# Attention in three layers: groups interleaved by a written order, ada steps moved into the product, filler matmuls on TensorE

## The chip, the cores and the metric

One Trainium2 chip, one of its cores. The engines are TensorE (PE), VectorE (DVE), ScalarE (ACT), GpSimd (POOL) and SyncE (SP, which here issues the weight loads). Each has its own queue that it works off in order; they meet only by semaphores. The metric is the device time of one execution in microseconds (us). TensorE's clock has two levels here, 1.2 and 2.4 GHz; a granted clock of 0.50 in the profile is the lower, 1.00 the upper.

## The reference, cut to what matters

The program is a chain of a block with two layers and a block with one, on 256 tokens of width 1024, all in float32:

```python
for l in range(2):                                    # first block
    mod = silu(c) @ ada_w[l] + ada_b[l]               # shifts, scales, gates
    hn = adaln(x, mix_norm_g[l], sh_m, sc_m)
    a_q, ..., d_v = split(hn @ w_in[l], IN_SPLITS)    # 1024 -> 3016
    o_a = diff_attention(...)             # A: p0 - lam*p1, then rmsnorm per head
    o_b = latent_attention(...)           # B: rmsnorm, @ w_uq, @ w_ukv, rope
    o_c = indexed_sparse_attention(...)   # C: index scores (I), top 64 keys, attention
    o_d = chunk_band_attention(...)       # D: banded bias
    x = x + g_m * (concat(o_a, o_b, o_c, o_d) @ w_out[l])
    x = x + g_f * (swiglu(...) if l == 0 else moe_swiglu(...))
x = rmsnorm(x, final_norm_g)
# second block: ffn1; qkv product; 8 heads of neighbourhood attention (N) and
# 8 of dilated attention (L); output product; ffn2
```

Each of A, B, C, D has 4 heads of 64 columns. A query block is 128 tokens; its keys are the first 128 or all 256.

## The kernel before, in words

**Weights.** Weight chunks of 1 MB come through a ring of six in one stream. A chunk is two pieces. For each piece ACT writes a rounded high part (`split_hi`, L988), DVE the low part (`split_lo`, L1411), and PE multiplies high*high, high*low and low*high (L527 to L529). Four pieces (`SPLITS`) are in work at once, so DVE can be that far ahead of PE. The products before attention are `gemm(0)`, `gemm(2)` and `gemm(4)`; the first runs from about 56 to 118.8 us.

**The modulation (ada).** 48 chunks of 1 MB are reduced on DVE by `ada_step` (L1324, L1327, L1330, two instructions each) into rows. POOL issues their loads (L444) into two slots of their own; a load waits until the step two before it has been done. Chunks 0 to 7 are done at the start, 8 to 25 inside attention 0, the rest in the first feed-forward part.

**Attention.** The work is cut into units: a kind (A, I, B, C, D in layers 0 and 1; N and L in the wide layer 2), a query block b and a part. A01 is kind A, block 0, part 1. Names that only have a kind and a number (C2, B6) are fills. A unit goes through:

- fill: PE transposes queries and keys into PSUM bank 7 (L642; for B also products, L678, L684), ACT copies them out (L1071);
- `score` on PE (L719), for one unit into one of two PSUM pairs;
- `bias` on DVE: scale and bias (L1497), row maximum (L1500);
- `probabilities` on ACT: four exponentials (L1117), for I a relu (L1112);
- for A the two parts are combined on DVE (`finish`, L1542, L1547); for I the weighted sum (`index_add`, L1511) and eight rounds of maximum and replace that select 64 keys (L1521, L1522);
- `values` on PE: transposes of the probabilities (L731), a copy by ACT (`copy_pT`, L1124), products with the values (L743);
- `store` on DVE (L1557; for A a norm with a root on POOL).

All engines run through one list of units: in each layer group A (A00 A01 A10 A11), then B, then C (I00 I01 I10 I11 C00 C10), then D. In each turn of PE's loop the score of the next unit stands before the values of this one; the fills of the next group stand around them. On DVE `prepare` and `prepare_rope` do the norms and rotations of the next group, and in layer 0 one ada step follows each unit. So at most one unit is ahead of the one whose values are being made.

## Time and profile before

| | us |
|---|---|
| median of 3 runs | 2490.25 (2489.54 to 2490.9) |
| profiled execution, device time | 2481.82 |
| its span | 2480.1 |
| PE busy | 2131.3 (86%) |
| DVE busy | 1693.4 (68%) |
| ACT busy | 1344.9 (54%) |
| POOL busy | 46.2 (2%) |

The page gives busy time by engine, then the span in 40 slices, of 62 us each. Slices 3 to 5 hold attention 0, 10 to 12 attention 1, and 35 and 36 the attention of layer 2. The long stretch of nines between is the experts. A matmul's end is modelled, so PE's busy time is a little more than its work. A PE row with `x8` is eight hardware records; four float32 matmuls of the program make eight.

### The profile page before, as it was taken

The numbers are of one execution on the slowest core, as the hardware profiler recorded it, in microseconds if no ns is written. First come the engines' busy times: TensorE is split into PE (matmuls) and PEld (weight loads), VectorE is DVE, ScalarE is ACT, GpSimd is POOL, SyncE is SP. The second block draws the span as 40 slices with busy tenths as digits, with TensorE's granted clock in tenths as the row PEclk, the third lists the DMA queues.
The fourth block names the chain that finished last, engine by engine and source line by source line (L and its number), as shares of the span: only waits on it lengthen the run. The fifth ranks groups of instructions, "written<-read, shape, count | busy, mean of one in ns | idle before, by whom it ended". The sixth has DMA issues, their size and how long they took to land.

```text
span 2480.1 us, 26703 instructions
## 1 busy us (share of the span) xinstructions
PE 2131.3 (86%) x9538; PEld 1735.1 (70%) x9538; DVE 1693.4 (68%) x2020; ACT 1344.9 (54%) x1832; POOL 46.2 (2%) x80
## 2 busy tenths in 40 slices
PE   3944779978657799999999999999969997866997
PEld 3733658866445688888888888888848885655886
DVE  5378377753463689898989898989975545344554
ACT  2422244434331687878787878787844434343443
POOL 1010000000000000000000000000000000000000
PEclk9956789989557899999999999999979998858999
DMA  9543358734003599999999999999954553202551
GB/s 374 180 152 104 130 208 314 308 140 159 0 15 146 214 358 353 351 353 351 353 351 354 352 356 349 355 349 356 373 204 169 189 182 120 84 17 86 202 186 51
DMA packets 80598, 573.41 MB, mean 231 GB/s; under 512 B 9088, under 2 KB 9728, under 8 KB 12272
## 3 DMA queue, kind: packets, MB, share of 16 engines
q1 hardware_dynamic: 70112, 508.59, 54.4%
q0 software_dynamic: 7936, 57.05, 6.2%
q10 hardware_dynamic: 2448, 6.41, 0.7%
q8 instruction: 63, 1.03, 0.2%
q14 instruction: 39, 0.32, 0.0%
HBM read 570.97 MB, written 1.05 MB: 231 GB/s over the span
## 4 chain that ended last, share of the span: by engine, by line
PE 73%; issue 12%; DVE 9%; ACT 3%; DMA 2%; POOL 1%; ACTq 0%; POOLq 0%; DVEq 0%
PE ps L527 21%; PE ps L529 21%; PE ps L528 21%; PE ps L743 2%; PE ps L719 2%; PE ps L822 1%; PE ps L829 1%; DMA arena<-in_ada 1%; PE ps L797 1%; PE ps L642 1%; DVE ps L1497 1%; DVE Z L1330 1%; PE ps L731 1%; DVE xt_low L1404 1%; DVE arena L1522 1%
## 5 line engine op out<-in xcount | busy, mean ns | idle before, releaser
L1670 DVE TENSOR_TENSOR weights_low<-ring,weights_high 128x1024 fp32r<-128x1024 f32 x672 | 803.8, 1224 | 63.1 <-ACT weights_high L1153 49.1
L1153 ACT ACTIVATE weights_high<-ring 128x1024 fp32r<-128x1024 f32 x672 | 710.5, 1060 | 105.4 <-PE ps L529 92.4
L527 PE MATMUL ps<-weights_high,xt_high 128*128 128x512 f32 x1808 | 729.7, 404 | 36.6 <-DVE xt_low L1404 24.7
L529 PE MATMUL ps<-weights_high,xt_low 128*128 128x512 f32 x1808 | 712.6, 394 | 0.0
L528 PE MATMUL ps<-weights_low,xt_high 128*128 128x512 f32 x1808 | 712.4, 394 | 0.0
L1411 DVE TENSOR_TENSOR weights_low<-ring,weights_high 128x1024 fp32r<-128x1024 f32 x294 | 357.7, 1224 | 244.0 <-ACT weights_high L988 242.5
L988 ACT ACTIVATE weights_high<-ring 128x1024 fp32r<-128x1024 f32 x294 | 307.3, 1057 | 335.9 <-PE ps L529 320.7
L527 PEld LDWEIGHTS ps<-weights_high,xt_high 128*128 128x128 f32 x1808 | 345.0, 191 | 110.8 <-DVE xt_low L1404 26.9
L529 PEld LDWEIGHTS ps<-weights_high,xt_low 128*128 128x128 f32 x1808 | 344.0, 190 | 73.7
L528 PEld LDWEIGHTS ps<-weights_low,xt_high 128*128 128x128 f32 x1808 | 345.5, 191 | 68.4 <-issue 1.0
L527 PE MATMUL ps<-weights_high,hT_high 128*128 128x512 f32 x712 | 283.4, 398 | 5.5 <-DVE hT_low L1448 4.2
L529 PE MATMUL ps<-weights_high,hT_low 128*128 128x512 f32 x712 | 277.3, 389 | 0.0
L528 PE MATMUL ps<-weights_low,hT_high 128*128 128x512 f32 x712 | 277.1, 389 | 0.0
L527 PEld LDWEIGHTS ps<-weights_high,hT_high 128*128 128x128 f32 x712 | 133.7, 188 | 36.9 <-DVE hT_low L1448 5.0
L528 PEld LDWEIGHTS ps<-weights_low,hT_high 128*128 128x128 f32 x712 | 133.7, 188 | 30.6 <-issue 3.4
L529 PEld LDWEIGHTS ps<-weights_high,hT_low 128*128 128x128 f32 x712 | 133.6, 188 | 28.1
L519 PE MATMUL ps<-unit,XN 128*128 128x128 f32 x160 | 36.5, 422 | 87.5 <-DVE XN L1378 80.4
L743 PE MATMUL ps<-arena 128*128 128x64 f32 x320 | 67.7, 395 | 34.8 <-ACT arena L1124 16.4
L519 PEld LDWEIGHTS ps<-unit,XN 128*128 128x128 f32 x160 | 32.7, 227 | 91.6 <-DVE XN L1378 83.8
L743 PEld LDWEIGHTS ps<-arena 128*128 128x128 f32 x320 | 63.6, 302 | 43.2 <-ACT arena L1124 30.1
L731 PE MATMUL ps<-unit,arena 128*128 128x128 f32 x160 | 36.1, 394 | 58.6 <-ACT arena L1117 43.4
L1117 ACT ACTIVATE arena<-ps,nmax 128x256 f32<-128x256 f32 (+1 forms) x112 | 47.1, 436 | 58.7 <-DVE nmax L1500 58.6
(192 smaller groups left out, 1474.1 us busy)
## 6 DMA issues: line engine op xcount, KB each, us to landing
ring<-in_stream SPq DMA_DIRECT2D x483, 1024.0 KB, 4.9
Z<-in_ada POOLq DMA_DIRECT2D x42, 1024.0 KB, 5.1
arena<-in_ada POOLq DMA_DIRECT2D x6, 1024.0 KB, 16.4
Z<-in_na POOLq DMA_DIRECT2D x1, 2048.0 KB, 7.8
Z<-in_dil POOLq DMA_DIRECT2D x1, 2048.0 KB, 12.2
band<-in_band ACTq DMA_DIRECT2D x2, 768.0 KB, 18.7
X<-in_x SPq DMA_DIRECT2D x1, 1024.0 KB, 5.4
gate_mix<-in_rows ACTq DMA_DIRECT2D x2, 512.0 KB, 9.6
```

Of the source, the lines that this page charges most:

```text
L519: m = nc.tensor.transpose(ps[:, j, (kt % 2) * T + b * P:(kt % 2) * T + (b + 1) * P], XN[:, b, kt * P:(kt + 1) * P], ident[:, :])
L527: nc.tensor.matmul(out, xh, wh, start=n, stop=False, skip_group_check=True)
L528: nc.tensor.matmul(out, xh, wl, start=False, stop=False, skip_group_check=True)
L529: return nc.tensor.matmul(out, xl, wh, start=False, stop=last, skip_group_check=True)
L719: m = nc.tensor.matmul(out, lhs, rhs, start=True, stop=True)
L731: m = nc.tensor.transpose(ps[:, 4 + h // 2, (h % 2) * T + kb * P:(h % 2) * T + (kb + 1) * P], src[:, head_slot(h), kb * P:(kb + 1) * P], i ...
L743: m = nc.tensor.matmul(ps[:, 6, h * HD:(h + 1) * HD], PT[:, h, kb, :], PROJ[:, kb, c:c + HD], start=kb == 0, stop=kb == u.nk // P - 1)
L988: act.activation(WH[:, p % SPLITS, :], ring[:, chunk % RING, half * PIECE:(half + 1) * PIECE], ACT.Copy).then_inc(hi_ready, 1)
L1117: ins = act.activation(PR[:, par, s, 0:u.nk], src[:, s, 0:u.nk], ACT.Exp, bias=nmax[:, par, s:s + 1], accum_out=den[:, par, h:h + 1])
L1153: act.activation(WH[:, slot, :], raw, ACT.Copy).then_inc(m["hi_ready"], 1)
L1411: nc.vector.tensor_tensor(WL[:, p % SPLITS, :], ring[:, chunk % RING, half * PIECE:(half + 1) * PIECE], WH[:, p % SPLITS, :].bitcast(F32), ...
L1670: nc.vector.tensor_tensor(WL[:, slot, :], raw, WH[:, slot, :].bitcast(F32), ALU.subtract).then_inc(m["lo_ready"], 1)
```

## The change

1. The rule that built one list of units is gone. PE, ACT and DVE each have a sequence written out by hand for layers 0 and 1, and a loop for layer 2. `Order` objects give every fill, score, transposition and so on its number within its semaphore. Groups now overlap: I (index scores) runs inside A, the selection of block 0 beside B's fills, B and D before C.
2. Scratch that groups shared gets places of its own in the x^T buffers, which are idle in attention (`xt_words`). PSUM stays as it was.
3. `values` is split into `turn` and `values`. Each has six bf16 matmuls of constants into parts of PSUM that nobody reads (`stay_busy`), before its last wait: 12 for each of 24 units, 288 in all.
4. Of the 18 ada steps of attention 0, 14 go into `gemm_lo(0)` on DVE: ten behind every second split, four behind the last.
5. `combine` folds the four scalings of p0 away: it forms p0 + p1 * (r1 * lam * den0), and the division by den0 is done at the store.
6. The memset of `KI4` goes from DVE to POOL. The A store's norm is cut in two (`store_squares`, `store_normed`) so that the root is not waited for.

```diff
 class Order:
+    def __call__(self, layer, name):
+        return self.start(layer) + self.names(layer).index(name) + 1
+FILLED = Order("A0 A1 C3 C2 B0 B1 B2 B3 B4 B5 C0 B6 B7 B8 B9 D0 D1 C1", "N00 N01 N10 N11 L00 L01 L10 L11")
+SCORED = Order("A00 A01 I00 I01 A10 A11 I10 I11 B00 B10 D00 D10 C00 C10", "N00 N10 N01 N11 L00 L10 L01 L11")
...
+            def stay_busy(count, bank):
+                for _ in range(count):
+                    nc.tensor.matmul(ps[:, bank, 256:512], busy[:, 0:P], busy[:, 0:256], start=True, stop=True,
+                                     skip_group_check=True)
...
+            def turn(layer, name):
+                if TURNED(layer, name) > 1:
+                    pe.wait_ge(pT_ready, TURNED(layer, name) - 1)
+                stay_busy(6, 5)
+                if u.kind == "A":
+                    pe.wait_ge(combined, COMBINED(layer, name))
+                else:
+                    pe.wait_ge(probs, WEIGHED(layer, name))
...
+            def values(layer, name):
+                if TURNED(layer, name) > 1:
+                    pe.wait_ge(mixed, TURNED(layer, name) - 1)
+                stay_busy(6, 6)
+                pe.wait_ge(pT_ready, TURNED(layer, name))
...
             def gemm_lo(g):
                 for p in range(SPLITS, 4 * GEMM_GROUPS[g]):
                     split_lo(GEMM_CHUNK[g] + p // 2, p % 2)
+                    if g == 0 and p % 2 == 1:
+                        ada_step(ADA_EARLY + (p - SPLITS) // 2)
+                if g == 0:
+                    lambda_sums()
+                    for a in range(2 * GEMM_GROUPS[g] - SPLITS // 2, ADA_IN_GEMM):
+                        ada_step(ADA_EARLY + a)
...
+            def combine(layer, b):
+                dve.wait_ge(probs, WEIGHED(layer, f"A{b}1"))
+                link(nc.vector.reciprocal(rden[:, 0, :], den[:, n1, :]))
+                link(nc.vector.scalar_tensor_tensor(rden[:, 0, :], rden[:, 0, :], lamc[:, 4 + layer:5 + layer], den[:, n0, :],
+                                                    ALU.mult, ALU.mult))
...
+            def attention(layer):                       # DVE, layers 0 and 1
+                prepare_index(layer)
+                more_ada(0)
+                bias(layer, "A00")
+                bias(layer, "A01")
+                norm_latent(layer)
+                more_ada(1)
+                if layer == 0:
+                    lambdas()
+                combine(layer, 0)
+                index_add(layer, "I00")
+                index_add(layer, "I01")
+                bias(layer, "A10")
+                store_squares(layer, "A01")
+                bias(layer, "A11")
+                rope_latent(layer)
+                combine(layer, 1)
+                select_keys(layer, 0)
...
+                select_keys(layer, 1)
+                store(layer, "B10")
+                bias(layer, "C00")
+                store(layer, "D00")
+                bias(layer, "C10")
+                store(layer, "D10")
+                more_ada(2)
+                store(layer, "C00")
+                more_ada(3)
+                store(layer, "C10")
```

Where the instructions stand. First DVE's queue where the first product ends and attention 0 begins (L1411 is a split, L1324, L1327 and L1330 are ada steps, L1497 and L1500 the bias of A00, L1360 and L1602 the norm of B), before:

```order
L1411 TENSOR_TENSOR weights_low<-ring,weights_high 128x1024 x22
...
L1782 TENSOR_SCALAR gdiff<-gdiff 128x64
L1497 SCALAR_TENSOR_TENSOR ps<-ps,alibi 128x4x128
L1500 TENSOR_REDUCE nmax<-ps 128x4
L1360 TENSOR_SCALAR rstd<-ss 128x2 x2
L1602 TENSOR_SCALAR arena<-arena,rstd 128x256 x2
L1602 TENSOR_SCALAR arena<-arena,rstd 128x128 x2
L1324 TENSOR_SCALAR Z<-Z,csilu 128x1024
L1330 SCALAR_TENSOR_TENSOR Z<-Z,csilu 128x1024
L1327 SCALAR_TENSOR_TENSOR Z<-Z,csilu 128x1024
L1330 SCALAR_TENSOR_TENSOR Z<-Z,csilu 128x1024
```

and in the changed kernel (L1497 is now the split, L1404, L1407 and L1410 the ada steps, L1706 and L1707 `prepare_index`, L1589 and L1592 the bias):

```order
L1497 TENSOR_TENSOR weights_low<-ring,weights_high 128x1024 x2
L1407 SCALAR_TENSOR_TENSOR Z<-Z,csilu 128x1024
L1410 SCALAR_TENSOR_TENSOR Z<-Z,csilu 128x1024
...
L1407 SCALAR_TENSOR_TENSOR Z<-Z,csilu 128x1024
L1410 SCALAR_TENSOR_TENSOR Z<-Z,csilu 128x1024
L1706 TENSOR_SCALAR w<-arena 128x8
L1707 COPY xt_words<-arena 128x128
L1706 TENSOR_SCALAR w<-arena 128x8
L1707 COPY xt_words<-arena 128x128
L1407 SCALAR_TENSOR_TENSOR Z<-Z,csilu 128x1024
L1410 SCALAR_TENSOR_TENSOR Z<-Z,csilu 128x1024
L1589 SCALAR_TENSOR_TENSOR ps<-ps,alibi 128x4x128
```

What moved: the splits have ada steps between them and behind them, and one more stands before the first bias; the long run of ada steps behind B's norm is gone.

Second, PE's queue in the last part of attention 0, from the scores of C (L719 score, L731 transposes, L743 values, L519 the transposes of the next product), before:

```order
L719 MATMUL ps<-arena 128x128 x4
L719 MATMUL ps<-arena 128x256 x4
L731 MATMUL ps<-unit,arena 128x128 x4
L743 MATMUL ps<-arena 128x64 x4
L719 MATMUL ps<-arena 128x128 x4
L731 MATMUL ps<-unit,arena 128x128 x8
L743 MATMUL ps<-arena 128x64 x8
L719 MATMUL ps<-arena 128x256 x4
L731 MATMUL ps<-unit,arena 128x128 x4
L743 MATMUL ps<-arena 128x64 x4
L731 MATMUL ps<-unit,arena 128x128 x8
L743 MATMUL ps<-arena 128x64 x8
```

and the end of the same part in the changed kernel (L482 `stay_busy`, L674 score, L689 transposes, L705 values, L490 as L519):

```order
L689 MATMUL ps<-unit,arena 128x128 x4
L674 MATMUL ps<-arena 128x128 x4
L482 MATMUL ps<-unit 128x256 x6
L689 MATMUL ps<-unit,arena 128x128 x8
L482 MATMUL ps<-unit 128x256 x6
L705 MATMUL ps<-arena 128x64 x4
L674 MATMUL ps<-arena 128x256 x4
L482 MATMUL ps<-unit 128x256 x6
L705 MATMUL ps<-arena 128x64 x8
L482 MATMUL ps<-unit 128x256 x6
L689 MATMUL ps<-unit,arena 128x128 x4
L482 MATMUL ps<-unit 128x256 x6
```

What moved: C is now last, and a score or another unit's step stands between the transposes and the values of nearly every unit, with six fillers before each.

Third, two turns of PE's loop in layer 2 (L642 and L603 are fills), before:

```order
L642 MATMUL ps<-unit,arena 128x128 x8
L731 MATMUL ps<-unit,arena 128x128 x8
L743 MATMUL ps<-arena 128x64 x8
L719 MATMUL ps<-arena 128x256 x4
L731 MATMUL ps<-unit,arena 128x128 x8
L743 MATMUL ps<-arena 128x64 x8
L719 MATMUL ps<-arena 128x256 x4
```

and now:

```order
L689 MATMUL ps<-unit,arena 128x128 x8
L674 MATMUL ps<-arena 128x256 x4
L603 MATMUL ps<-unit,arena 128x128 x4
L482 MATMUL ps<-unit 128x256 x6
L705 MATMUL ps<-arena 128x64 x8
L482 MATMUL ps<-unit 128x256 x6
L689 MATMUL ps<-unit,arena 128x128 x8
L674 MATMUL ps<-arena 128x256 x4
L603 MATMUL ps<-unit,arena 128x128 x4
L482 MATMUL ps<-unit 128x256 x6
L705 MATMUL ps<-arena 128x64 x8
```

What moved: the score now stands behind the transposes of a unit two earlier, no longer one.

## Rows read from the trace of the kernel before

**Rows 1.** The page: granted clock in tenths, in 40 slices.

```profile
PEclk9956789989557899999999999999979998858999
```

**Rows 2.** Windows (us): busy time of each engine; attention 0, 1, 2, first product.

```profile
core 0: us, PE busy (x) PEld busy (x) DVE busy (x) ACT busy (x) POOL busy (x), PEclk, DMA share, GB/s
56.00:118.80 62.80, 62.75 (x277) 51.63 (x275) 25.48 (x25) 26.07 (x31) 0.00 (x0) 1.00 0.51 186
118.80:270.00 151.20, 75.38 (x320) 55.44 (x320) 103.98 (x215) 41.59 (x126) 12.76 (x21) 0.56 0.36 130
607.70:736.70 129.00, 73.28 (x321) 55.23 (x321) 60.79 (x173) 41.53 (x126) 3.02 (x3) 0.60 0.02 6
2127.00:2216.30 89.30, 69.87 (x332) 57.33 (x330) 25.04 (x33) 31.17 (x86) 0.00 (x0) 0.67 0.04 13
```

**Rows 3.** Timeline: start us, us, engine line op; in brackets idle before; layer 1.

```profile
701.38 1.11 PE L731 MATMUL ps<-unit,arena 128*128 128x128 f32 x4 [8.73 <-ACT arena L1117]
...
724.56 1.23 DVE L1497 SCALAR_TENSOR_TENSOR ps<-ps,band 128x1024 f32<-128x1024 f32 x1 [8.20 <-PE ps L719]
```

**Rows 4.** Timeline: where attention 1 and attention 2 begin.

```profile
607.73 1.09 ACT L1008 ACTIVATE arena<-ps 128x512 f32<-128x512 f32 x2 [8.85 <-PE ps L529]
...
612.85 0.70 DVE L1497 SCALAR_TENSOR_TENSOR ps<-ps,alibi 128x512 f32<-128x512 f32 x1 [13.68 <-PE ps L719]
...
2138.04 0.66 PE L642 MATMUL ps<-unit,arena 128*128 128x128 f32 x4 [1.18 <-ACT arena L1008]
```

**Rows 5.** DVE's groups of attention 0: count, busy us, mean ns, idle before.

```profile
L1330 DVE SCALAR_TENSOR_TENSOR Z<-Z,csilu 128x1024 f32<-128x1024 f32 x18 | 23.1, 1285 | 0.6
L1327 DVE SCALAR_TENSOR_TENSOR Z<-Z,csilu 128x1024 f32<-128x1024 f32 x13 | 16.7, 1285 | 3.3 <-DMA Z<-in_ada 2.8
...
L1324 DVE TENSOR_SCALAR Z<-Z,csilu 128x1024 f32<-128x1024 f32 x5 | 3.8, 751 | 2.8 <-DMA Z<-in_ada 2.7
```

**Rows 6.** DMA issues of the whole span: count, KB each, median us to landing.

```profile
Z<-in_ada POOLq DMA_DIRECT2D x42, 1024.0 KB, 5.1
arena<-in_ada POOLq DMA_DIRECT2D x6, 1024.0 KB, 16.4
```

**Rows 7.** DVE's groups of attention 1.

```profile
L1542 DVE TENSOR_SCALAR arena<-arena,rden 128x256 f32<-128x256 f32 x4 | 1.1, 347 | 0.0
...
L1542 DVE TENSOR_SCALAR arena<-arena,rden 128x128 f32<-128x128 f32 x4 | 0.9, 281 | 0.0
```

**Rows 8.** Timeline of PE: values, scores and transposes at both levels of the clock.

```profile
660.75 3.67 PE L743 MATMUL ps<-arena 128*128 128x64 f32 x16 [1.11 <-ACT arena L1124]
...
682.06 2.00 PE L743 MATMUL ps<-arena 128*128 128x64 f32 x16 [1.11 <-ACT arena L1124]
...
2173.80 1.13 PE L719 MATMUL ps<-arena 64*128 64x256 f32 x8
2174.86 1.09 PE L731 MATMUL ps<-unit,arena 128*128 128x128 f32 x8
...
2181.27 2.08 PE L719 MATMUL ps<-arena 64*128 64x256 f32 x8
...
2192.62 2.08 PE L719 MATMUL ps<-arena 64*128 64x256 f32 x8
```

**Rows 9.** Timeline of PE: two passes of a weight product at half clock.

```profile
746.07 0.63 PE L529 MATMUL ps<-weights_high,xt_low 128*128 128x512 f32 x1
746.50 0.63 PE L527 MATMUL ps<-weights_high,xt_high 128*128 128x512 f32 x1
```

**Rows 10.** Windows of 4 us in attention 1 (columns as in rows 2).

```profile
628.00:632.00 4.00, 3.72 (x8) 1.95 (x10) 0.00 (x0) 0.98 (x5) 0.00 (x0) 0.50 0.00 0
632.00:636.00 4.00, 3.07 (x10) 0.99 (x8) 2.88 (x5) 1.93 (x9) 0.00 (x0) 0.95 0.00 0
...
664.00:668.00 4.00, 4.00 (x13) 3.17 (x13) 0.01 (x1) 0.00 (x0) 0.00 (x0) 0.50 0.00 0
...
696.00:700.00 4.00, 0.00 (x0) 0.00 (x0) 3.82 (x7) 0.18 (x1) 0.00 (x0) 0.50 0.00 0
```

More of the change, by code:

```diff
@@ L166, with __init__, names, start @@
-GROUPS, UNITS = attention_plan()
+    def __init__(self, kind, b, part):
+        self.kind, self.b, self.part = kind, b, part
+        self.name = f"{kind}{b}{part}"
+        self.half = part if kind in "NL" else 0
+        self.nk = T if kind in "NL" else P * (b + 1)
+UNIT = {u.name: u for kind in "ABICDNL" for b in range(NB) for part in range(2) for u in [Unit(kind, b, part)]}
+class Order:
+    def __init__(self, early, late=""):
+        self.early, self.late = early.split(), late.split()
+    def names(self, layer):
+        return self.early if layer < LAYERS else self.late
+    def start(self, layer):
+        return layer * len(self.early)
+    def end(self, layer):
+        return self.start(layer) + len(self.names(layer))
+    def __call__(self, layer, name):
+        return self.start(layer) + self.names(layer).index(name) + 1
@@ L167, with place @@
+COMBINED = Order("A01 A11")
+INDEXED = Order("I00 I01 I10 I11")
+def place(layer, name):
+    return SCORED.names(layer).index(name)
 N_CONST = 8
@@ L486, in _ @@
             root(0, 2)
-            attention_roots()
+            pool.wait_ge(gemm_out, 2 * sum(GEMM_GROUPS[:2]) + 2)
+            pool.memset(KI4, 0.0).then_inc(ki_cleared, 1)
+            root(0, 4)
+            for b in range(NB):
+                root(4, 8)
             pool.wait_ge(mod_ready, 12)
@@ L747, in attention @@
             def attention(layer):
-                us = units_of(layer)
                 pe.wait_ge(gemm_out, 2 * sum(GEMM_GROUPS[:2 * layer + 1]))
-                fills(us[0].g, 0, us[0].g.n_fills)
-                score(us[0])
-                for n, u in enumerate(us):
-                    part = fill_part(u)
-                    if part and last_of_group(u):
-                        fills(*part)
-                    if n + 1 < len(us):
-                        score(us[n + 1])
-                    if part and not last_of_group(u):
-                        fills(*part)
-                    if u.pu is not None:
-                        values(u)
+                fill(layer, "A0")
@@ new lines, in attention @@
+                fill(layer, "A1")
+                score(layer, "A00")
+                fill_index_keys(layer)
+                score(layer, "A01")
+                fill(layer, "C2")
+                fill(layer, "B0")
+                score(layer, "I00")
+                score(layer, "I01")
+                fill_latent_keys(layer)
+                turn(layer, "A01")
+                latent_queries(layer, 0)
+                score(layer, "A10")
+                latent_queries(layer, 1)
+                values(layer, "A01")
@@ new lines, in attention @@
+                score(layer, "B10")
+                fill(layer, "D1")
+                values(layer, "A11")
+                score(layer, "D00")
+                turn(layer, "B00")
+                score(layer, "D10")
+                values(layer, "B00")
+                turn(layer, "B10")
+                fill(layer, "C1")
+                values(layer, "B10")
+                turn(layer, "D00")
+                score(layer, "C00")
+                turn(layer, "D10")
+                values(layer, "D00")
@@ new lines, in attention @@
+                rope_latent(layer)
+                combine(layer, 1)
+                select_keys(layer, 0)
+                index_add(layer, "I10")
+                store_normed(layer, "A01")
+                index_add(layer, "I11")
+                bias(layer, "B00")
+                bias(layer, "B10")
+                store_squares(layer, "A11")
+                bias(layer, "D00")
+                store_normed(layer, "A11")
+                bias(layer, "D10")
+                store(layer, "B00")
```

622 lines of the change are left out of this document (310 added, 312 removed).

## The prediction

> **What bounds the kernel now.** I read the page first: engine shares and slices. PE is busy 86% of the span, and the slices in which it is not are few; in the same slices the granted clock drops [rows 1]. I then cut the time into stretches by a table of windows. The first weight product (56 to 118.8 us) is bound by PE: 62.75 of 62.8 us at full clock, DVE only 25.48 us busy, DMA share 0.51. The three attention stretches are bound by nothing for long: in layer 0 PE is busy 75.38 of 151.2 us, DVE 103.98, ACT 41.59; in layer 1 PE 73.28 of 129, DVE 60.79, ACT 41.53; and the granted clock averages 0.56 and 0.60, mostly the 1.2 GHz level [rows 2]. The timeline of layer 1 shows why: units take turns. While DVE does the key selection of C, PE stands idle 8.73 us, and soon afterwards DVE waits 8.20 us for the next score [rows 3]. So latency of one unit after another bounds these stretches, and a slow PE is in that chain. The windows of layers 0 and 1 begin with the product's last copy (1.09 us) and end with the last store; behind the copy they last 151.2 - 1.1 = 150 and 129.0 - 1.1 = 128 us, and layer 2 from its first fill at 2138.0 to 2216.3, 78 us [rows 2, 4]; together 356. All other stretches keep their instructions.
>
> **Part 1: 14 ada steps leave attention 0.** There 18 steps stand in DVE's queue: 23.1 + 16.7 + 3.8 = 43.6 us, 2.4 us each, and 2.8 + 2.7 us of waits for their loads [rows 5]. Four stay. Fourteen (34 us) go into the first product: ten behind every second split, four behind the last. The product asks DVE for 25.48 us in 62.8, so one step per pair of splits gives 2 x 1.23 + 2.4 = 4.9 us of DVE per 24 matmuls of 62.75/277 = 0.227 us, that is 5.4 us of PE [rows 2]: it fits by 0.5 us, and SPLITS = 4 pieces stand between DVE and PE. The cover is thin but real. The DMA share would be 0.51 + about 0.5. An ada load lands after 5.1 us (median of 42 here) and has two step periods less a step, 10.9 - 2.4 = 8.5 us, to do so; the bound above is the 16.4 us of the first six loads, which were issued together [rows 6]. I take the 5.1, and 2 us of loss in the product for contention (range 0 to 40, below).
> The four steps behind the last split are not covered. Two ring slots and 5.1 + 2.4 us per pair of steps make about 3.8 us a step: DVE comes to the first bias of attention 0 about 8 us late, and to the first combine about 10 us late (a fifth step, more_ada(0), also waits for its load). ACT's exponentials and I00's score wait behind that combine. Of the other steps, more_ada(1) is inside that figure and the last two stand in gaps at the end. Cost: 10 us.
>
> **Part 2: the new orders, layer 1, by DVE's queue.** Head: bias A00 starts 4.0 us after the copy as now (612.85 against 607.73 + 1.09) [rows 4]; then A00's and A01's exponentials, the combine and the two relus pass through one after another, and DVE starts index_add(I00) about 14.5 us after the copy (my estimate from the same operations' durations). From there DVE's queue has work that is ready nearly always: the scores are issued one or two units earlier, and the selections, the rope and the squares fill what were waits. DVE's 60.79 us of now [rows 2] lose the eight scalings of combine, 1.1 + 0.9 us [rows 7], the memset that moves to POOL and two copies: about 57. About 6 of these stand in the head, so 51 follow, plus some 2 us of issue gaps and one wait: 53. Tail behind bias C10: four exponentials, transposes, copy, values, store, 7.5 us at full clock. Sum 14.5 + 53 + 7.5 = **75 us, if PE runs at 2.4 GHz**.
> Does PE fit? Its 73.28 us at a mean clock of 0.60 are 44 us at full clock [rows 2], and the prices confirm the factor of nearly two: values 3.67 against 2.00 us, scores 2.08 against 1.13 [rows 8]. The new filler matmuls have no row. A 128x256 bf16 pass has half the columns of the 512-column passes: 0.227/2 = 0.113 us at full clock, and (746.50 - 746.07)/2 = 0.21 us at 1.2 GHz [rows 2, 9]; it could cost as little as nothing, where it lies in a wait, and 0.43 if width did not matter. I take 0.113 and 0.21. 96 of them are 11 or 20 us a layer. PE: 44 + 11 = 55 us of 75 at full clock, under DVE; but 88 + 20 = 108 at half clock, over DVE, and with the head's idle time the stretch is then 114.
> Which clock? From 628 to 632 us PE was busy 3.72 of 4 us at 0.50, and in the next 4 us the clock was 0.95; at 696 to 700 PE was idle and it was 0.50 again [rows 10]. In the new order PE has its gaps in the head (clock falls, as now) and from some 16 us on is busy 70 to 100%: at half clock it saturates, so the clock rises; at full clock it waits for DVE a quarter of the time and may fall again. I take 10 us over the 75: **85 us, a gain of 43** (bounds: 53 and 14).
> Layer 0 is the same plus the 10 us of part 1: **95 us against 150, a gain of 55** (bounds 65, 26).
>
> **Part 3: layer 2.** Now a unit takes 11.35 us (score to score at half clock: 2181.27 to 2192.62 [rows 8]). The new loop scores two units ahead, so PE never waits for an exponential: per unit at full clock transposes 1.09, score 1.13, fill 0.66 (first four units), values 2.00 [rows 4, 8] and fillers 12 x 0.113: 6.2 us with a fill, 5.6 without, a little less where ends overlap. ACT, by my estimate 4.7 us a unit, is shorter. A head of 9 us, the units (5.9 and 5.3 us, the last two without a score), a tail of 4: 52 us. At 1.2 GHz the sum per unit is 2.0 + 2.08 + 1.1 + 3.67 + 12 x 0.21 = 11.4, no shorter than today, and the stretch would take 91. PE without gaps should get its clock; I allow 4 us for the start: **56 us against 78, a gain of 22** (bounds 26 and -13).
>
> **Sum.** 55 + 43 + 22 - 2 = 118 us. Profiled execution 2481.8 - 118 = 2363.8. The median of the runs shown is 2490.25, 8.4 us above that execution, so the same gain gives **2372 us**. About 5 us (0.2%) is what can be told from no change.
>
> **A rule against the change.** The Trainium skill (TensorE: Matmul & The Clock Gate, Part 4, PE-mode transpose) says that transposes don't count as PE activity for the clock gate; fills and turns are transposes here, so less of PE's work would hold the clock than its busy time suggests. By that rule the time is the first rival's, 2465; by the busy rows it is 2372. No row here separates the two: most stretches hold both kinds.
>
> **Rivals.**
> - *The clock stays at 1.2 GHz* (20%). PE becomes the bound with its fillers on top: 124, 114 and 91 us for the three stretches, 329 against 356: gain 27, less 2: 2465. For: at 664 to 668 us PE was busy 4.00 of 4 us and the clock stayed at 0.50 [rows 10]. Against: gaps end now every busy spell, and the new queues leave hardly any.
> - *The clock stays up* (17%): 85, 75, 52 us: gain 144, less 2: 2348.
> - *Ada loads crowd the first product* (6%). If they land after 16.4 us [rows 6], a step takes (16.4 + 2.4)/2 = 9.4 us against 5.4 of PE: ten steps hold the splits 40 us, five more cost some 20: gain 58, 2432.
> - *Slower* (4%): the order hides nothing, since three in-order queues with cross waits merely exchange which engine stands; then all 288 fillers lie on the path at 1.2 GHz, 288 x 0.21 = 61 us, against 34 us of ada steps gone: 27 slower, 2517. It decides where the new overlap saves less than 27 us in three stretches. Against it: the idle times of rows 3 have nothing behind them but order.
> - *No net change* (2%): a mix of the two before.
>
> **How the numbers follow.** My forecast has 51%, around 2372 with its own range of 2350 to 2400. The five cases above take the rest. Eight in ten: from 2340 (full clock and a little) to 2445 (crowded loads, part of the low-clock case). Faster by over 0.2%: 0.51 + 0.20 + 0.17 + 0.06 and nearly nothing else, 0.94; same 0.02; slower 0.04.
>
> **What would show it.** Windows of the three stretches: lengths near 95, 85, 56 us; DVE busy near 70 us of layer 0 and 57 of layer 1, over two thirds of each; granted clock above 0.8 from 16 us into each. No PE wait over 3 us on DVE's selection. In the first product DVE busy near 50 us with PE still near 100%; a wait of DVE on the ada DMA just before prepare_index. I am wrong if the fillers are at 0.21 us and PE is busy all of the attention, if the first product is over 5 us longer, or if DVE still waits for scores in the middle of the stretches.

## The result, and the profile after

| | before | changed kernel |
|---|---|---|
| median of 4 runs each, same chip | 2489.89 us (2485.77 to 2490.9) | 2347.64 us (2345.06 to 2348.61) |
| ratio | | 0.943, 95% interval 0.9414 to 0.9446 |
| profiled execution, its span | 2481.82, 2480.1 us | 2348.61, 2346.6 us |

The predicted time was 2372 us, with a range of 2340 to 2445; the likeliest case's own range of 2350 to 2400 was missed by 2 us, on the fast side. The rival "the clock stays up" had said 2348.

The page's clock line, after, answers to [rows 1]:

```profile
PEclk9978799988979999999999999999979998987999
```

The table of windows, after: the three attention stretches, each from the end of the last copy of the product ahead of it to the end of its last store:

```profile
core 0: us, PE busy (x) PEld busy (x) DVE busy (x) ACT busy (x) POOL busy (x), PEclk, DMA share, GB/s
119.87:209.17 89.30, 63.07 (x416) 50.20 (x416) 72.35 (x183) 39.45 (x125) 7.83 (x11) 0.83 0.24 85
549.12:626.51 77.39, 61.00 (x416) 49.28 (x416) 56.86 (x164) 39.12 (x124) 3.02 (x3) 0.89 0.03 9
2028.23:2081.36 53.13, 47.47 (x384) 39.99 (x384) 23.70 (x32) 28.92 (x81) 0.00 (x0) 0.97 0.00 1
```

Measured in the same way the kernel before has 150.1, 127.8 and 78.3 us at clocks of 0.56, 0.59 and 0.63 (the longer windows of [rows 2]). The three gains are 60.8, 50.4 and 25.2 us, 136.4 in all; the profiled executions differ by 133.2, so the rest of the program is 3 us longer (1.1 us between attention 0 and 1, 0.4 between 1 and 2, 1.4 behind 2; why is not shown). The first product still ends its last copy at 119.87 us, as before, though DVE and the DMA engines have much more to do in it. Over the 62.8 us of [rows 2] DVE is now busy 51.12 us (it was 25.48) and the DMA share is 0.91 (it was 0.51). Its last three slices of 20 us:

```profile
60.00:80.00 20.00, 20.00 (x90) 16.58 (x89) 17.58 (x15) 9.40 (x12) 1.64 (x3) 1.00 0.85 327
80.00:100.00 20.00, 20.00 (x89) 16.55 (x89) 17.10 (x16) 9.56 (x12) 2.11 (x4) 1.00 0.99 385
100.00:120.00 20.00, 18.75 (x83) 15.22 (x82) 16.37 (x19) 6.22 (x9) 2.11 (x4) 1.00 0.95 369
```

Behind it stands the tail of ada steps. The timeline of DVE: where the last two steps of the tail begin, the step behind `prepare_index` (`more_ada(0)`), the first bias:

```profile
121.75 0.75 DVE L1404 TENSOR_SCALAR Z<-Z,csilu 128x1024 f32<-128x1024 f32 x1 [1.14 <-DMA Z<-in_ada]
...
129.70 1.28 DVE L1407 SCALAR_TENSOR_TENSOR Z<-Z,csilu 128x1024 f32<-128x1024 f32 x1 [5.88 <-DMA Z<-in_ada]
...
132.64 1.28 DVE L1407 SCALAR_TENSOR_TENSOR Z<-Z,csilu 128x1024 f32<-128x1024 f32 x1
...
135.15 0.69 DVE L1589 SCALAR_TENSOR_TENSOR ps<-ps,alibi 128x512 f32<-128x512 f32 x1
```

The bias starts 15.3 us behind the product's end. In the kernel before these were 4.3 us (124.13 less 119.87).

The wait of 5.88 us is for the load that POOL issued at 120.91 us. The rows of that issue and of the times to landing of the ten loads from 95 to 150 us:

```profile
120.91 0.53 POOL L410 DMA_DIRECT2D Z<-in_ada  x1 [3.73 <-DVE Z L1410]
...
DMA to landing us min/median/max: 4.9/5.1/8.8
```

120.91 + 8.8 is 129.7, where the step begins: this load took 8.8 us to land and not 5.1. ACT had issued a load of 384 KB (`in_uq`) at 120.29 us, which took 9.2 us (3.3 before). So some 3.7 us of the late start look like loads in each other's way; no run separates that.

What bounds layer 1 now? The timeline of DVE: three waits of the head, then every row that begins with an idle time of 0.2 us or more, and the row maximum of the last bias (start us, us, engine, line, operation; in brackets the idle time and who ended it):

```profile
553.74 0.70 DVE L1589 SCALAR_TENSOR_TENSOR ps<-ps,alibi 128x512 f32<-128x512 f32 x1 [4.08 <-PE ps L674]
...
560.61 0.18 DVE L1626 RECIPROCAL rden<-xt_words 128x4 f32<-128x4 f32 x1 [1.40 <-ACT arena L1151]
...
566.08 0.35 DVE L1606 SCALAR_TENSOR_TENSOR xt_words<-arena,w,cmask 128x128 f32<-128x128 f32 x1 [3.85 <-ACT arena L1146]
...
588.49 0.48 DVE L1606 SCALAR_TENSOR_TENSOR xt_words<-arena,w,cmask 128x256 f32<-128x256 f32 x1 [0.60 <-ACT arena L1146]
...
615.32 1.23 DVE L1589 SCALAR_TENSOR_TENSOR ps<-ps,alibi 128x1024 f32<-128x1024 f32 x1 [0.23 <-PE ps L674]
...
617.85 1.22 DVE L1592 TENSOR_REDUCE nmax<-ps 128x4 f32<-128x1024 f32 x1
...
621.45 0.42 DVE L1646 TENSOR_TENSOR XN<-ps,rden 128x256 f32<-128x256 f32 x1 [1.75 <-PE ps L705]
...
626.09 0.42 DVE L1646 TENSOR_TENSOR XN<-ps,rden 128x256 f32<-128x256 f32 x1 [4.13 <-PE ps L705]
```

From the first index_add (566.08) to the end of the last bias (619.07) DVE waits 0.83 us in 53.0. The waits of 8 to 9 us of [rows 3] are gone; PE's longest wait in this stretch is now one of 2.98 us:

```profile
580.02 0.64 PE L603 MATMUL ps<-unit,arena 128*96 128x128 f32 x4 [2.98 <-DVE xt_words L1689]
```

What is left is a head of 17.0 us and a tail of 7.4 us in which the units pass through one by one. The windows of head, dense part and tail show where the clock is low:

```profile
549.12:566.08 16.96, 12.61 (x65) 10.35 (x66) 5.98 (x21) 10.91 (x38) 1.01 (x1) 0.60 0.12 39
566.08:619.07 52.99, 42.54 (x302) 33.67 (x301) 49.35 (x139) 24.95 (x78) 2.01 (x2) 0.97 0.01 1
619.07:626.51 7.44, 5.85 (x50) 5.26 (x50) 1.53 (x7) 3.26 (x10) 0.00 (x0) 1.00 0.00 0
```

The clock is 0.60 in the head and 0.97 in the dense part, in which PE is busy 42.5 of 53.0 us.

Layer 2, the timeline of PE, one unit and the start of the next (L482 the fillers):

```profile
2061.87 1.04 PE L689 MATMUL ps<-unit,arena 128*128 128x128 f32 x8
2062.84 1.13 PE L674 MATMUL ps<-arena 64*128 64x256 f32 x8
2063.90 0.83 PE L482 MATMUL ps<-unit 128*128 128x256 bf16 x6
2064.57 1.90 PE L705 MATMUL ps<-arena 128*128 128x64 f32 x16
2066.30 0.82 PE L482 MATMUL ps<-unit 128*128 128x256 bf16 x6
2066.96 1.04 PE L689 MATMUL ps<-unit,arena 128*128 128x128 f32 x8
```

No row has an idle time in front: here PE is the bound, with 5.09 us a unit (it was 11.35 at half clock, [rows 8]). Of them 0.67 + 0.66 us are fillers (from the start of a group of six to the next row), 0.11 us for each filler. (A row's own 0.82 us overlaps the next one.)

### The profile page after: what moved, and what is told of

Its sections match the earlier page's. It is cut to its first block, busy times and chain, and to the rows that moved or that the text cites. A ratio compares the mean times of both kernels' runs of the same rounds, so it can differ in the third digit from the quotient of the medians.

```text
span 2346.6 us, 27245 instructions
## 1 busy us (share of the span) xinstructions
PE 2094.9 (89%) x9826; PEld 1714.2 (73%) x9826; DVE 1683.8 (72%) x2002; ACT 1342.4 (57%) x1832; POOL 48.1 (2%) x82
## 4 chain that ended last, share of the span: by engine, by line
PE 74%; issue 12%; DVE 8%; DMA 2%; ACT 2%; POOL 1%; ACTq 0%; POOLq 0%; DVEq 0%
PE ps L498 22%; PE ps L500 22%; PE ps L499 22%; PE ps L838 1%; PE ps L674 1%; PE ps L845 1%; DMA arena<-in_ada 1%; PE ps L813 1%; PE ps L705 1%; DVE xt_low L1490 1%; PE ps L603 1%; PE ps L482 1%; DVE ps L1589 1%; DMA Z<-in_ada 1%; DMA Z<-in_dil 1%
## 5 line engine op out<-in xcount | busy, mean ns | idle before, releaser
L1497 DVE TENSOR_TENSOR weights_low<-ring,weights_high 128x1024 fp32r<-128x1024 f32 x294 | 357.5, 1223 | 227.8 <-ACT weights_high L1004 226.4
L490 PE MATMUL ps<-unit,XN 128*128 128x128 f32 x160 | 34.4, 404 | 87.5 <-DVE XN L1464 80.1
L490 PEld LDWEIGHTS ps<-unit,XN 128*128 128x128 f32 x160 | 31.1, 217 | 91.4 <-DVE XN L1464 83.6
L1024 ACT ACTIVATE arena<-ps 128x512 f32<-128x512 f32 x48 | 25.7, 586 | 68.7 <-PE ps L500 68.7
L1242 ACT ACTIVATE hT_high<-ps 128x256 fp32r<-128x256 f32 x112 | 42.8, 382 | 37.7 <-PE ps L813 37.7
L1042 ACT ACTIVATE FS<-ps 128x512 f32<-128x512 f32 x33 | 19.7, 598 | 76.5 <-PE ps L500 76.5
L1812 DVE TENSOR_TENSOR hT_low<-ps,hT_high 128x256 fp32r<-128x256 f32 x112 | 46.9, 418 | 22.9 <-ACT hT_high L1242 22.9
## 6 DMA issues: line engine op xcount, KB each, us to landing
arena<-in_ada POOLq DMA_DIRECT2D x6, 1024.0 KB, 16.2
```

The lines of the kernel that those rows point to most:

```text
L490: m = nc.tensor.transpose(ps[:, j, (kt % 2) * T + b * P:(kt % 2) * T + (b + 1) * P], XN[:, b, kt * P:(kt + 1) * P], ident[:, :])
L1024: act.activation(dst[:, b, q * 512:(q + 1) * 512], ps[:, 4 + 2 * (q % 2) + b, :], ACT.Copy).then_inc(gemm_out, 1)
L1242: act.activation(hTH[:, par].rearrange("p f n -> p (f n)"), ps[:, 6 + par, 0:2 * P], ACT.Copy).then_inc(m["hT_hi"], 1)
L1497: nc.vector.tensor_tensor(WL[:, p % SPLITS, :], ring[:, chunk % RING, half * PIECE:(half + 1) * PIECE], WH[:, p % SPLITS, :].bitcast(F32), ...
L1812: nc.vector.tensor_tensor(hTL[:, par].rearrange("p f n -> p (f n)"), ps[:, 6 + par, 0:2 * P], hTH[:, par].rearrange("p f n -> p (f n)").bi ...
```

## Experiments

Each group of runs has its own runs of the kernel before on its chip (medians 2484.9 to 2489.9 us), and a ratio is to those. Ratios of different chips carry some 0.2% of their own: experiment 4 has the changed kernel's time within 0.2 us, but 0.9453 for 0.943, since the kernel before was 5 us faster on that chip. So small differences are read from the times and the stretches too. "Stretches" are attention 0, 1 and 2 as above. My theory: order and clock together, the order hiding latencies and the fillers holding the clock. Rivals: the order alone, the clock alone.

**1. The changed kernel without the fillers.**

```diff
             def stay_busy(count, bank):
-                for _ in range(count):
-                    nc.tensor.matmul(ps[:, bank, 256:512], busy[:, 0:P], busy[:, 0:256], ...)
+                pass
```

> The changed kernel without its 288 filler matmuls (they write to PSUM that nobody reads, so the result is the same). Three theories of the 142 us that the change gained. Theory 1, order and clock together: the fillers hold TensorE at 2.4 GHz while it waits for DVE, and without them the granted clock of the three attention stretches falls back from 0.88 towards the 0.6 of before; each of the two DVE-bound stretches loses 5 to 15 us, layer 2 about 5: 2360 to 2385 us. Theory 2, order alone: the dense queue holds the clock by itself; then the fillers only cost, at least the 96 x 0.11 = 10.6 us of layer 2, where PE has no gaps: 2337 us or a little less, clock still near 0.9. Theory 3, clock alone: nearly all of the gain is the fillers' and the time goes back above 2440. I hold theory 1, with 2370.

Measured: 2353.89 us, ratio 0.9475 (0.9462 to 0.9488). The windows:

```profile
119.21:213.53 94.32, 63.27 (x320) 50.76 (x320) 74.12 (x184) 39.66 (x125) 7.82 (x11) 0.70 0.25 89
553.10:633.12 80.02, 60.37 (x320) 48.41 (x320) 56.99 (x164) 39.19 (x124) 3.02 (x3) 0.75 0.03 9
2034.52:2086.51 51.99, 41.54 (x288) 33.73 (x288) 23.73 (x32) 28.92 (x82) 0.00 (x0) 0.86 0.00 1
```

Clocks fall from 0.83, 0.89, 0.97 to 0.70, 0.75, 0.86: the fillers do hold the clock. But it falls only halfway to that of before, and the time rises by little: 5.0 and 2.6 us in layers 0 and 1, and 1.1 us less in layer 2. The fillers are worth 6 us by the times and by the stretches (0.25%), and 0.45% by the ratios, out of 5.7%. No theory's number came out. Theory 1 had 2360 to 2385, with a clock near 0.6, and I held 2370; theory 2 had 2337 with a clock near 0.9. The fillers' part is real and small, and nearly all of the gain needs no filler.

**2. The kernel before with only the ada move** (ten steps in `gemm_lo(0)`, four behind `lambdas()`, just ahead of attention 0; loads issued accordingly, that part is left out here).

```diff
                     split_lo(GEMM_CHUNK[g] + p // 2, p % 2)
+                    if g == 0 and p % 2 == 1:
+                        ada_step(ADA_EARLY + (p - SPLITS) // 2)
...
-                    if g.layer == 0:
-                        for a in range(ADA_EARLY, ADA_EARLY + ADA_IN_B):
-                            ada_step(a)
...
                 if layer == 0:
                     lambdas()
+                    for a in range(10, ADA_IN_GEMM):
+                        ada_step(ADA_EARLY + a)
```

> The kernel before with one part of the change: 14 of the 18 ada steps go from attention 0 into the first product (ten behind every second split, four behind the last); order of the groups and everything else as before, no fillers. In the kernel before, attention 0 is 150 us and attention 1 is 128 us with the same units, so the 18 steps cost 22 us of 43.6 us of work. If the steps left in the tail cost the 10 us that I counted, 14/18 x 22 - 10 = 7 us are gained: 2483 us of 2490. If the tail is hidden in the old order (its head waits for PE and ACT anyway), up to 17 us: 2473. If the steps lie wholly on the path in the old order, 34 - 10 = 24 us: 2466. I hold 2480; the share of this part in the whole gain is then under a tenth.

Measured: 2475.66 us, ratio 0.9965 (0.9951 to 0.9978). Attention 0 is 142.8 us, from 150.1; the others are within 0.7 us of before. The 7.3 us are the 7 of my expectation's sum; in the medians it is 9.

**3. The kernel before with only the fillers.**

```diff
             def values(u):
+                stay_busy(6, 5)
                 ... (wait for probs or combined, transposes)
-                pe.wait_ge(pT_ready, u.pu + 1)
                 if u.pu >= 1:
                     pe.wait_ge(mixed, u.pu)
+                stay_busy(6, 6)
+                pe.wait_ge(pT_ready, u.pu + 1)
```

> The kernel before with the 12 fillers of each unit alone: six before the wait for the probabilities (or the combine), six before the wait for the transposed probabilities; one wait, for the store of the unit before, stands ahead of the second six. Order as before. Theory 1 (order and clock together): the waits of the old order are 4 to 9 us long and six fillers fill 0.7 to 1.3 us of them, so the clock rises only here and there: mean of the stretches from 0.60 to perhaps 0.70, some 10 to 20 us gained less some us of fillers on the path: 2475 to 2490. Theory 3 (clock alone): the stretches go to 0.85 or more and 60 us or more are gained: under 2430. Theory 2 (order alone): the fillers only cost, 288 x 0.11 to 0.21 us, up to 61 us where they delay the next step: 2490 to 2550. I hold 2485.

Measured: 2465.42 us, ratio 0.9923 (0.9908 to 0.9938). Its windows, and two rows of PE's timeline in layer 1:

```profile
120.19:268.61 148.42, 77.83 (x416) 58.38 (x416) 103.96 (x215) 40.51 (x125) 12.74 (x21) 0.69 0.36 132
609.15:727.79 118.64, 74.56 (x416) 55.07 (x416) 60.79 (x173) 40.42 (x124) 3.02 (x3) 0.73 0.02 6
2131.22:2199.87 68.65, 52.92 (x384) 43.92 (x384) 23.82 (x32) 29.06 (x82) 0.00 (x0) 0.90 0.00 1
```

```profile
694.75 1.11 PE L739 MATMUL ps<-unit,arena 128*128 128x128 f32 x4 [7.98 <-ACT arena L1126]
709.12 1.97 PE L739 MATMUL ps<-unit,arena 128*128 128x128 f32 x8 [9.30 <-ACT arena L1126]
```

The clock goes from 0.56, 0.59, 0.63 to 0.69, 0.73, 0.90 and the stretches lose 1.7, 9.2 and 9.7 us: in the old order a faster PE is worth something in every unit's turn, most in layer 2, where PE is most of the turn. The long waits for DVE's selection stay: 7.98 and 9.30 us, where they were 8.73 [rows 3] and 9.45. I held 2485 and had 2475 to 2490 for theory 1: too little, by what layer 2 gains. So the fillers alone bring 0.8%. By subtraction (experiment 1 less the ada move of experiment 2) the order brings 4.9%, with all that goes with it: DVE also loses 3.9 us of work in layer 1 (60.79 to 56.86), in `combine` and the memset above all, and no run has the order without these, or without the ada move. The parts overlap: in the new order the same fillers bring only 0.25 to 0.45%.

**4. One ada step moved by one place.**

```diff
                 prepare_index(layer)
-                more_ada(0)
...
                 norm_latent(layer)
+                more_ada(0)
                 more_ada(1)
```

> The changed kernel with the fifteenth ada step moved from ahead of the first bias to behind the norm of B's inputs, next to the sixteenth. It waits 5.88 us for its load there and takes 2.4 us. If DVE's late start is on the path of attention 0, the first bias comes up to 8 us sooner, the first combine 0 to 8 us sooner (the step's wait only moves behind bias A01 if ACT's exponentials take less time than the two steps): gain 2 to 8 us, 2340 to 2346. If something else (PE's clock in the head, ACT) sets the start of the dense part, no change: 2348. I hold 2344.

Measured: 2347.85 us, ratio 0.9453 (0.9437 to 0.9469): no gain. Its first bias and first combine on DVE:

```profile
131.17 0.69 DVE L1589 SCALAR_TENSOR_TENSOR ps<-ps,alibi 128x512 f32<-128x512 f32 x1
...
143.78 1.14 DVE L1632 SCALAR_TENSOR_TENSOR arena<-arena,rden 128x128 f32<-128x128 f32 x4
```

Behind the end of the product (119.39 us here) the bias comes at 11.8 us, 3.5 sooner, but the combine at 24.4 against 24.5 (144.33 less 119.87 in the changed kernel). My expectation had put the wait of 5.88 us on the wrong step: the rows above show that the step I moved (132.64) waits for nothing, and that it is the last one of the tail, ahead of it, that waits. I expected 2344, and 2348 if nothing changed. The moved step's 2.5 us stand ahead of the combine in either place.

**5. Another filler: transposes.**

```diff
-                for _ in range(count):
-                    nc.tensor.matmul(ps[:, bank, 256:512], busy[:, 0:P], busy[:, 0:256], ...)
+                for _ in range(count * 2 // 3):
+                    nc.tensor.transpose(ps[:, bank, 256:384], ident[:, :], ident[:, :])
```

> The changed kernel with another kind of filler: each group of six bf16 matmuls of constants becomes four float32 transposes of a constant (0.66 us at full clock by the rows of the real transposes, as the six took). They write where nobody reads. This tells the Trainium skill's rule (TensorE: Matmul & The Clock Gate, Part 4) that transposes don't count as activity for the clock gate apart from the rival that any busy TensorE holds the clock. By the rule the transposes cost time and hold nothing: granted clocks of the three stretches as without fillers (0.70, 0.75, 0.86) or below, 2354 us plus up to 10 for layer 2: 2354 to 2366. By the rival they do what the matmuls do: clocks of 0.83, 0.89 and 0.97, and 2348 us. I hold neither firmly; the real transposes ran at 272 ns nearly throughout in the changed kernel, so the rival 60 to 40.

Measured: 2345.77 us, ratio 0.9422 (0.9406 to 0.9438).

```profile
119.46:212.07 92.61, 62.82 (x384) 50.95 (x384) 74.10 (x184) 39.44 (x125) 7.83 (x11) 0.80 0.24 85
552.46:628.09 75.63, 56.56 (x384) 46.37 (x384) 56.90 (x164) 39.18 (x123) 3.02 (x3) 0.91 0.03 10
2030.65:2081.53 50.88, 44.60 (x352) 37.75 (x352) 23.73 (x32) 28.93 (x82) 0.00 (x0) 0.97 0.01 1
```

Clocks of 0.80, 0.91, 0.97, against 0.70, 0.75, 0.86 with no filler: float32 transposes hold the clock nearly as the matmuls do. Over the whole program the runs agree: 0.945 to 0.947, against 0.948 to 0.950 with matmuls and 0.931 to 0.937 with no filler. The Trainium skill (TensorE: Matmul & The Clock Gate, Part 4) says that the full clock does not engage for transposes on TensorE, as such a transpose "doesn't count as PE-busy the same way"; its figures there are for bf16. For these float32 transposes, among other work of TensorE, that does not hold, and the measurement decides. I had put their price at 0.66 us a group; the timeline shows 0.50 (a group starts at 2062.46, the next row at 2062.96), which explains layer 2: 16 groups at 0.16 us less are 2.6 us, and it is 2.2 us shorter. Attention 0 is 3.3 us longer than with matmuls, at a clock 0.03 lower, and experiment 9 shows the same (2.7 us, 0.80 against 0.86); why is not shown.

**6. Twice the fillers** (24 a unit: `range(2 * count)`).

> The changed kernel with 24 fillers a unit instead of 12. Without fillers the three stretches lasted 94.3, 80.0 and 52.0 us, with 12 they last 89.3, 77.4 and 53.1. Theory: in layers 0 and 1 DVE is the bound and the fillers lie in PE's waits, in layer 2 PE is the bound and they lie on the path. Then doubling adds 96 x 0.11 = 10.6 us to layer 2 (63 to 64 us; 24 fillers less where they fill its head), and in layers 0 and 1 the clock goes up by a few hundredths and the time by -2 to +3 us each: PE's work is then 61 + 11 = 72 us of 77 to 89, so it begins to be late for DVE. Total 2356 to 2365; I hold 2359. Rival, that fillers are free everywhere (a wait always covers them): 2346 to 2350. Rival, that PE is already at its limit in all three: 3 x 10.6 = 32 more, 2380.

Measured: 2364.58 us, ratio 0.9505 (0.9491 to 0.952).

```profile
119.79:212.86 93.07, 70.75 (x512) 58.65 (x512) 72.87 (x183) 39.63 (x125) 7.84 (x11) 0.85 0.24 83
553.29:635.96 82.67, 70.47 (x512) 58.60 (x512) 57.03 (x164) 39.28 (x123) 3.02 (x3) 0.90 0.03 9
2038.28:2098.36 60.08, 55.98 (x480) 48.48 (x480) 23.74 (x32) 28.97 (x82) 0.00 (x0) 1.00 0.01 1
```

The clock barely rises (0.85, 0.90, 1.00) and the stretches grow by 3.8, 5.3 and 7.0 us. 96 fillers of 0.11 us are 10.6 us: two thirds of it is on the path in layer 2, and between a third and a half in layers 0 and 1. So in layers 0 and 1 PE's work is not simply hidden behind DVE's, as I had it (I held 2359, in 2356 to 2365); and neither rival holds, that fillers are free everywhere (2346 to 2350) or wholly on the path everywhere (2380).

**7. Half the key selection** (32 keys instead of 64, so it leaves out half of that part of the computation).

```diff
-                for r in range(N_SEL // 8):
+                for r in range(N_SEL // 16):
```

> The changed kernel with four rounds of the key selection instead of eight: 32 keys are taken and not 64, so this part of the computation is changed. In attention 1 the 16 rounds take DVE 5.8 + 5.5 + 1.5 = 12.8 us (maximum, replace and its value load, busy time); half of them is 6.4 us a layer. If DVE is the bound of the stretches of layers 0 and 1 (its queue waits 0.83 us in all between the first index_add and the last stores of layer 1), the whole 12.8 us come off: 2335 us, 83 and 71 us for the two stretches. If PE's values and scores are as late as DVE (two engines near their limit), about half: 2341. If latency through all the engines still bounds it, nearly nothing: 2347. I hold 2336.

Measured: 2342.33 us, ratio 0.9413 (0.9395 to 0.943). The window of layer 1, DVE's row that answers to 588.49 of the changed kernel, and ACT's relu that it waits for:

```profile
546.38:621.28 74.90, 59.41 (x416) 48.47 (x416) 50.76 (x140) 39.07 (x124) 3.02 (x3) 0.91 0.03 10
```

```profile
584.88 0.48 DVE L1606 SCALAR_TENSOR_TENSOR xt_words<-arena,w,cmask 128x256 f32<-128x256 f32 x1 [3.38 <-ACT arena L1146]
583.75 1.02 ACT L1146 ACTIVATE arena<-ps 128x1024 f32<-128x1024 f32 x1 [4.22 <-PE ps L689]
```

DVE has 56.86 - 50.76 = 6.1 us less to do, the stretch is 2.5 us shorter. The wait for block 1's first relu (L1146) is now 3.38 us instead of 0.60: 2.8 us of the selection of block 0 turned into a wait for the relu, which itself waits for PE. So DVE's queue without gaps is one of two chains that are nearly equally late. Layer 0 shows the same (86.0 instead of 89.3 us, 0.6 us of it ahead of the first combine and so not the selection's). I had held 2336, for all of DVE's saving on the path; the case "about half", 2341, is the one that came.

**8. The ada steps of the tail spread over attention 0.** The last step of the tail goes behind B's norm, the two behind it go behind the first combine and behind the index_add of I00. POOL issues their loads accordingly (left out here).

```diff
-                    for a in range(2 * GEMM_GROUPS[g] - SPLITS // 2, ADA_IN_GEMM):
+                    for a in range(2 * GEMM_GROUPS[g] - SPLITS // 2, ADA_IN_GEMM - 1):
...
                 prepare_index(layer)
-                more_ada(0)
...
                 norm_latent(layer)
-                more_ada(1)
+                more_ada(-1)
...
                 combine(layer, 0)
+                more_ada(0)
                 index_add(layer, "I00")
+                more_ada(1)
```

> The changed kernel with the last ada step of the first product's tail moved behind the norm of B's inputs, and the two steps behind it into later places (behind the first combine and behind the first index_add), so that no step stands where its load has just been issued. Moving one step by one place changed nothing, since the two steps of the tail that wait for loads (2.94 and 3.93 us) stood as before, and the combine came at 143.3 us. If DVE's serial work from the first combine on is the bound of attention 0, each us of load wait that goes comes off the end: the first bias at about 125 us instead of 131, the first combine at about 133, two steps more of DVE work (5 us) behind it: a gain of 3 to 6 us, 2342 to 2345. If PE or ACT (its clock in the head) is the bound, no change, 2347 to 2348; the loads themselves may also be late in the new places, 2347. I hold 2343.5.

Measured: 2343.71 us, ratio 0.9417 (0.9404 to 0.943). The window of attention 0, and DVE's first bias and first combine in it:

```profile
119.45:201.95 82.50, 62.65 (x416) 50.12 (x416) 73.87 (x184) 39.54 (x124) 7.85 (x11) 0.86 0.28 97
```

```profile
125.14 0.69 DVE L1589 SCALAR_TENSOR_TENSOR ps<-ps,alibi 128x512 f32<-128x512 f32 x1
...
135.03 1.14 DVE L1632 SCALAR_TENSOR_TENSOR arena<-arena,rden 128x128 f32<-128x128 f32 x4
```

Counted from the product's end (119.45), the bias comes at 5.7 us, 9.6 sooner, and the combine at 15.6, 8.9 sooner; the three moved steps now wait for no load (of the tail that is left, one waits 3.02 us). The stretch is 6.8 us shorter; 1.0 us of it is lost in layer 1 (78.4 us, clock 0.87). I held 2343.5. By the ratios (0.9417, 0.943) the intervals still overlap.

**9 and 10. Combinations.** The spread ada steps with transposes as fillers; and with half of the bf16 fillers (`range(count // 2)`).

> The two edits that came out at least as fast as the changed kernel, together: the ada steps spread into later places (2343.7 us alone), and four float32 transposes for each group of six bf16 fillers (2345.8 us alone; a group takes 0.50 us on TensorE's queue instead of 0.66, layer 2 was 50.9 us instead of 53.1). If they add, 2347.6 - 3.9 - 1.9 = 2342 us; attention 0 was 3.3 us longer with the transposes, layer 1 1.8 us shorter, so this may be clock chance: if only layer 2 counts, 2341.5; if the loss of attention 0 stays with the new order of ada steps, 2344.5. I hold 2342.

> The ada steps spread into later places, and three bf16 fillers a group instead of six (144 in all). With 0, 12 and 24 fillers a unit the stretches were 94.3/80.0/52.0, 89.3/77.4/53.1 and 93.1/82.7/60.1 us, so the optimum of layers 0 and 1 lies between 0 and 24, that of layer 2 near 0 to 12. If fillers are paid only for the clock and half of them holds it (0.80 or more), they save 0.33 us a group in layer 2, 16 groups: 5 us less there, and 0 to 3 us less in each of the others: 2336 to 2339. If half of them lets the clock fall to halfway of the kernel without fillers (0.77, 0.82), the savings are given back: 2343 to 2347. I hold 2341.

Measured: 2340.64 us, ratio 0.9405 (0.9388 to 0.9421), with stretches of 85.2, 75.7 and 50.8 us; and 2343.14 us, ratio 0.9412 (0.9392 to 0.9431), with 83.3, 79.2 and 50.1. With six fillers a unit the clocks are 0.83, 0.85 and 0.97, so half of them hold most of the clock, and what they save (3 us in layer 2) is given back in part in the others. I held 2342 and 2341. The kernel with the spread steps and the transposes has the lowest median of all, 7 us under the changed kernel's; from the half fillers it can't be told apart, and against the changed kernel its interval ends just above where the other's begins (0.9421, 0.9414).

## Why the prediction was right, and where it was not

**The bound and the mechanism: right.** The attention stretches were bound by latency, unit after unit, and the new order takes most of it away: without a filler the three stretches are 356.2 - 226.3 = 129.9 us shorter, of the 136.4 with fillers (experiment 1), the ada move's 7 among them.

**Layer 1, by DVE's queue: right in its terms, wrong in what I put on top.** Head 14.5, DVE 53, tail 7.5, 75 us in all, were measured as 17.0, 53.0 and 7.4, 77.4 us. The step that failed is the next one: "I take 10 us over the 75", for a clock that may fall again where PE "waits for DVE a quarter of the time". PE was idle a fifth of the dense part and the clock there was 0.97; it was low only in the head (0.60). The stretch is 2.4 us over the 75 in all, and the head is 2.5 of it. Even with no fillers and a clock of 0.75 layer 1 takes 80.0 us and not 85. Of the signs that I named, the clock above 0.8 from 16 us on held (0.87, 0.97 and 1.00 in the three stretches). The same 10 us stood in layer 0 (95 against 89.3 measured) and 4 us in layer 2 (56 against 53.1). Together the three stretches were forecast 5.7 + 7.6 + 2.9 = 16.2 us too long, and 24 us of the forecast were such allowances.

**PE's cover: half right.** It fits, and its work is as forecast (61.0 us at a clock of 0.89 are 54 at full clock), but the margin that "55 us of 75" suggested was not there: PE was busy 61 us of 77. Experiments 6 and 7 show that a us more of PE or a us less of DVE each moves the end by a third to a half. DVE was not the only bound, though its queue alone gave nearly the right length.

**The fillers' price: right where it could be read, and it mattered little.** 0.113 us was forecast, 0.11 measured. They are on the path of layer 2 and yet nearly cost nothing there (53.1 against 52.0 us), since the clock goes from 0.86 to 0.97.

**The ada move: right.** The product did not grow (0 against 2 us): DVE was busy 16.4 to 17.6 of every 20 us beside a full PE. A load still landed after 5.1 us in the median. The tail is a little longer than I said: the first bias, "about 8 us late", was 11.0, and layer 0 is 11.9 us longer than layer 1 against 10 forecast. The term that was too small is the landing, 8.8 us for the load of the tail's last step where I had 5.1. The step "more_ada(0), also waits for its load" was wrong: it waits for nothing, since the one before it waits 5.88 us and its own load lands in the meantime. And I took the tail as the price of the move; it is the price of the place, since spreading three steps gives 6.8 us of attention 0 back (experiment 8).

**Layer 2: nearly right, by a sum that does not add up.** A unit without a fill was forecast at 5.6 us and is 5.09: the sum took whole durations, and transposes, score and values overlap the next row by 0.07 to 0.17 us. But a head of 9, four units of 5.9 and four of 5.3 with two scores less (42.5), and a tail of 4 make 55.5 us and not 52; only with the last unit counted as the tail does it come near 52. Measured are 9.7 us to the first unit's transposes, 42.9 for the eight units (the first, partly at half clock, took 7.2) and 0.5 behind them, 53.1 in all. That "52 + 4" lies only 2.9 us off is in part luck.

**The offset: wrong.** I carried over the 8.4 us between the profiled execution of before and its median. The changed kernel's profiled execution is 1.0 us above its median, so 9.4 us of the error of 24.6 are this. Runs of the kernel before lie anywhere from 2481 to 2492 us; its profiled execution was at the low end, and that says nothing of another kernel.

The sum of it: 16.2 us in the stretches, 2 for the product, 9.4 for the offset, less 3 us that the rest of the program grew, is 24.6; 2372.2 - 2347.6 is the same.

**The rivals.** "Clock stays at 1.2 GHz" failed, and not for want of fillers: even without them the clock was 0.70, 0.75 and 0.86. The transposes' rule, which had the same 2465, failed with it (experiment 5). "Clock stays up" was nearer than my own case, with 85, 75 and 52 us for the stretches. But its 2348 is partly luck: its stretches are 7.8 us too short and it knew nothing of the 3 us of the rest, and the offset (9.4) and the 2 us for the product made up for both. Loads did not crowd the product (they did delay one step behind it), and the fillers did not lie on the path as a whole.

## What to carry to other kernels

Where several engines wait in turn, price the new order by the queue of the busiest engine (head, its work, tail): that gave layer 1 to 2.4 us, while the allowances for the clock, added by feel, were more than the whole error of the stretches. Then ask at what distance the second engine follows, since here a gain on one of two nearly equal chains was worth less than half. Fillers paid little once the order was dense, and a load that is waited for in an in-order queue costs by its place: move the step to where its load has had time.

## What the runs showed of the hardware

- Float32 transposes of a constant held the granted clock nearly as bf16 matmuls did (0.80, 0.91 and 0.97, against 0.83, 0.89 and 0.97 with matmuls and 0.70, 0.75 and 0.86 with no filler).
- Averaged over a stretch, the granted clock is far from all or nothing: with 0, 6, 12 and 24 fillers a unit layer 1 had 0.75, 0.85, 0.89 (0.87 in another run of the same queue) and 0.90.
- A denser queue raises the clock by itself, here by half to two thirds of what it rose in all: 0.70, 0.75 and 0.86 without fillers, against 0.56, 0.59 and 0.63 in the old order with the same matmuls (0.83, 0.89 and 0.97 with fillers).
- The first product ran at full speed with DMA shares of 0.85 to 0.99 (327 to 385 GB/s), against 0.51 before [rows 2]; 1 MB loads were not slower in the median (5.1 us in both kernels, [rows 6]), but one just behind the product took 8.8 us.
